# Low parts of two value-weight units formed by accumulating transfers in place of VectorE differences

## The reference, cut to what matters

```python
xn = rmsnorm(x, ln_g)
proj = xn @ w_in
q, k, v, z_a, x_b, z_b, g_a, g_b = jnp.split(proj, SPLIT_IDX, axis=-1)
q = rope(q.reshape(B, L, RET_HEADS, RET_DK), pos)
k = rope(k.reshape(B, L, RET_HEADS, RET_DK), pos) * (RET_DK ** -0.5)
v = v.reshape(B, L, RET_HEADS, RET_DV).astype(jnp.float32)
```

## Time and profile before

| | |
|---|---|
| median of 3 runs | 1920.78 us (1920.63 to 1921.49) |
| the profiled execution | 1921.01 us, of it the span 1919.2 us |
| TensorE busy | 1898.3 us, 99% of the span |
| VectorE, ScalarE, GpSimd busy | 1190.7, 771.4 and 267.1 us |
| mean granted TensorE clock | 0.998 |

### The profile page before, as it was taken

How to read it: one execution, slowest core, us unless ns; L and a number is a source line. 1 busy time by engine, 2 the same in 40 slices (tenths; PEclk the granted TensorE clock), 3 DMA queues, 4 the chain that set the end, 5 groups by cost and what they waited for, 6 DMA issues and landing times.

```text
span 1919.2 us, 32122 instructions
## 1 busy us (share of the span) xinstructions
PE 1898.3 (99%) x13128; PEld 1778.4 (93%) x13128; DVE 1190.7 (62%) x2024; ACT 771.4 (40%) x1205; POOL 267.1 (14%) x377
## 2 busy tenths in 40 slices
PE   8999999999999999999999999999999999999998
PEld 7889898898899999999998988988988999999997
DVE  8775665665766887424487656657557578763345
ACT  5432332323436776422344323234133377754223
POOL 2220120120232200000022201202102422000000
PEclk9999999999999999999999999999999999999999
DMA  6435544453453333322255445534543533342222
GB/s 217 133 118 165 171 136 129 159 179 116 138 158 97 108 99 119 103 78 78 88 172 157 143 126 170 176 113 144 171 130 126 164 108 105 92 138 79 88 79 81
DMA packets 105857, 246.99 MB, mean 129 GB/s; under 512 B 10830, under 2 KB 51262, under 8 KB 105326
## 3 DMA queue, kind: packets, MB, share of 16 engines
q1 hardware_dynamic: 78590, 149.71, 25.1%
q0 software_dynamic: 26976, 95.22, 15.0%
q10 hardware_dynamic: 144, 0.00, 0.0%
HBM read 186.07 MB, written 49.12 MB: 123 GB/s over the span
## 4 chain that ended last, share of the span: by engine, by line
PE 87%; DVE 5%; ACT 3%; DMA 1%; DVEq 1%; issue 1%; ACTq 1%; SPq 0%
PE bank L1679 22%; PE bank L1681 21%; PE bank L1680 21%; PE bank L1749 4%; PE bank L1751 4%; PE bank L1750 4%; PE last L1767 1%; PE last L1749 1%; PE last L1750 1%; PE last L1751 1%; PE sums L1874 1%; PE sums L1878 1%; PE sums L1876 1%; PE sums L1785 1%; PE bank L1932 1%
## 5 line engine op out<-in xcount | busy, mean ns | idle before, releaser
L1679 PE MATMUL bank<-xn_hi,w_hi 128*128 128x296 f32 (+1 forms) x2432 | 726.5, 299 | 0.1
L1681 PE MATMUL bank<-xn_lo,w_hi 128*128 128x296 f32 (+1 forms) x2432 | 722.3, 297 | 0.0
L1680 PE MATMUL bank<-xn_hi,w_lo 128*128 128x296 f32 (+1 forms) x2432 | 721.5, 297 | 0.0
L1679 PEld LDWEIGHTS bank<-xn_hi,w_hi 128*128 128x128 f32 x2432 | 457.3, 188 | 6.3 <-issue 4.3
L1680 PEld LDWEIGHTS bank<-xn_hi,w_lo 128*128 128x128 f32 x2432 | 457.7, 188 | 1.0
L1681 PEld LDWEIGHTS bank<-xn_lo,w_hi 128*128 128x128 f32 x2432 | 456.8, 188 | 0.0
L474 DVE TENSOR_TENSOR w_lo<-w_raw,w_hi 128x1024 fp32r<-128x1024 f32 x245 | 300.4, 1229 | 185.6 <-ACT w_hi L466 179.1
L466 ACT ACTIVATE w_hi<-w_raw 128x1024 fp32r<-128x1024 f32 x245 | 257.8, 1055 | 355.8 <-DMA w_raw<-in_w_units 351.4
L1679 PE MATMUL bank<-oa_hi,w_hi 128*128 128x296 f32 (+1 forms) x512 | 153.7, 300 | 0.0
L1680 PE MATMUL bank<-oa_hi,w_lo 128*128 128x296 f32 (+1 forms) x512 | 151.9, 297 | 0.0
L1681 PE MATMUL bank<-oa_lo,w_hi 128*128 128x296 f32 (+1 forms) x512 | 151.7, 296 | 0.0
(11 more groups left out here) (296 smaller groups left out, 3064.6 us busy)
## 6 DMA issues: line engine op xcount, KB each, us to landing
w_raw<-in_w_units SPq DMA_DIRECT2D x215, 512.0 KB, 3.6
S<-in_state_ret POOLq DMA_DIRECT2D x64, 512.0 KB, 4.8
out_ret_s<-S POOLq DMA_DIRECT2D x64, 512.0 KB, 6.0
w_raw<-in_w_units SPq DMA_DIRECT2D x66, 256.0 KB, 3.2
vst<-v_scr SPq DMA_DIRECT2D x8, 512.0 KB, 4.1
out_ret_p<-Sp POOLq DMA_DIRECT2D x8, 512.0 KB, 5.6
v_scr<-vtok_hi SPq DMA_DIRECT2D x16, 160.0 KB
dec<-in_decay POOLq DMA_DIRECT2D x9, 264.0 KB, 5.0
```

The lines of the kernel that those rows point to most:

```text
L1679: pe.matmul(ps, w_hi[:, slot, cols], x_hi, start=first, stop=False)
L1680: pe.matmul(ps, w_lo[:, slot, cols], x_hi, start=False, stop=False)
L1681: return pe.matmul(ps, w_hi[:, slot, cols], x_lo, start=False, stop=last)
```

## The change

For units 4 and 5 of the first head of the first layer alone, the low part is made in another way. After making the high part, ScalarE drains and writes the negated high part into `w_lo`. GpSimd then issues two transfers for each unit, with the same strided source as the load of `w_raw`, that add the raw weights from memory to what stands in `w_lo` (raw + (-high) = low). VectorE's `split_lo` for these units makes no difference any more; it waits for both transfers and then counts `unit_lo` up. GpSimd issues unit 4's transfers behind the four state loads, and unit 5's between the low parts of input blocks 1 and 2 (`k == 2`), each after waiting for the negated part.

```diff
+        BY_SUM = (4, 5)
+
+        def by_sum(ph, l, it, i):
+            return ph == "R" and (l, it) == (0, 0) and i + AHEAD in BY_SUM
+
         def split_hi(act, ph, l, it, i):
...
             act.activation(w_hi[:, n % RING, :], w_raw[:, n % RING, :], ACT.Copy).then_inc(unit_hi, 1)
+            if by_sum(ph, l, it, i):
+                act.drain()
+                act.activation(w_lo[:, n % RING, :], w_hi[:, n % RING, :].bitcast(f32), ACT.Copy, scale=-1.0)\
+                   .then_inc(minus_hi, 1)
+
+        def add_raw(pool, u):
+
+            pool.wait_ge(minus_hi, BY_SUM.index(u) + 1)
+            if is_value(u):
+                n = u % 16 - 4
+                for i in range(2):
+                    k = 2 * n + i
+                    pool.dma_start(w_lo[:, u % RING, i * DV:i * DV + DV].rearrange("p (c w) -> p c w", c=4),
+                                   w_units[u - n:u - n + 4, :, k * P:k * P + P].rearrange("c p w -> p c w"),
+                                   accum_op=ADD).then_inc(lo_in[BY_SUM.index(u)], 16)
...
         def split_lo(dve, ph, l, it, i):
...
+            if by_sum(ph, l, it, i):
+                dve.wait_ge(lo_in[BY_SUM.index(n)], 32 if is_value(n) else 16)
+                dve.sem_inc(unit_lo, 1)
                 return
...
                     for n in range(S_RING):
                         load_state(n)
+                    if hh == 0:
+                        add_raw(pool, BY_SUM[0])
                     if h == 0:
                         for k in range(KT):
+                            if hh == 0 and k == 2:
+                                add_raw(pool, BY_SUM[1])
                             pool.wait_ge(xnh_ready, l * KT + k + 1)
```

More of the change, by code:

```diff
@@ L369, in trunk @@
             "const_in", "trig_in", "ones_ready", "x_ready", "x_stored", "x_again"))
-        gain_in = sem("gain_in")
+        gain_in, minus_hi, lo_in = sem("gain_in"), sem("minus_hi"), [sem(f"lo_in{i}") for i in range(2)]
         xgh_ready, xg_ready = sem("xgh_ready"), sem("xg_ready")
@@ L466, in split_hi @@
             act.activation(w_hi[:, n % RING, :], w_raw[:, n % RING, :], ACT.Copy).then_inc(unit_hi, 1)
+            if by_sum(ph, l, it, i):
[11 more added lines that the diff above has]
+                                   accum_op=ADD).then_inc(lo_in[BY_SUM.index(u)], 16)
+            else:
+                pool.dma_start(w_lo[:, u % RING, :], w_units[u], accum_op=ADD).then_inc(lo_in[BY_SUM.index(u)], 16)
         def split_lo(dve, ph, l, it, i):
@@ L471, in split_lo @@
             if l * UNITS_LAYER + it * p.units + p.unit0 + n >= UNITS:
+                return
+            if by_sum(ph, l, it, i):
+                dve.wait_ge(lo_in[BY_SUM.index(n)], 32 if is_value(n) else 16)
+                dve.sem_inc(unit_lo, 1)
                 return
```

## The result

The changed kernel takes 1925.02 us (median of 11 runs, 1923.58 to 1926.50) against 1920.78 before (11 runs, 1920.22 to 1921.49): 4.2 us more, ratio 1.0025 with a 95% interval of 1.0017 to 1.0032. That is a loss, at the edge of the 0.2% that I called no change. Its first state load starts at 23.91 us against 23.55 before, so its start was 0.36 us slower for reasons outside the change; this is taken off where positions are compared.

A forecast was written before the change was run, and what follows sets the result against it. TensorE, 99% busy, was taken to bound the kernel, with 2.2 us of gaps to win. Unit 5's landing at 46.4 starts VectorE's normalisation late (44.01 before), transposes 2.4 us late: 1920.8 becomes 1923.2 us, range 1919.8 to 1927.5.

The forecast's parts named there:

- the forecast: Unit 5's transfers land at 46.4 (44.0 to 47.8), clock full, transposes 2.4 us late: 1923.2 us; chance 0.42.
- rival 2: TensorE idles 3.9 us before the third value block and its clock falls: +2.1, together +4.5, 1925.3 us; chance 0.14.
- What bounds: TensorE, 99% busy; VectorE's first normalisation at 44.01 fixes the transposes 6.17 us later, so a delay there is paid in full.
- ScalarE's copies: One added copy per unit, about 1.2 us with the drain, lies in ScalarE's idle time and costs nothing.
- Unit 4: Its transfers land by 36.9, VectorE asks at 39.9: hidden; a 1.2 us difference comes off VectorE.
- The issues: GpSimd issues unit 5's two transfers at 38.9 and 39.6, 0.71 us each, holding nobody else.
- one of my signs of being wrong: On GpSimd, the forecast is wrong if the issues take much longer than 0.7 us each.
- The landing of unit 5: Where VectorE waits: 39.6 + 3.4 + 1.7 + 1.7 = 46.4, bounds 42.3 to 49.2.
- the shared engines: Unit 7's loads, issued at 40.54, share the transfer engines and delay unit 5's landing by 1.7 us, between nothing and 1.8.
- the addition: Reading the target as well as the source delays unit 5's landing by 1.7 us, between nothing and 1.8.
- rival 1: Unit 5's addition is slow, a third of a copy's rate: landing from 47.8, loss over 0.2%, up to 1926.0; chance 0.24.
- The clock's price: At 1.2 GHz the 12 remaining value products take 2.8 us more, less 0.7 slack before the transposes: +2.1 us.

The follow-up runs named there:

- second group: Later experiments on one chip, beside 27 runs of the kernel before (1920.90 us), including the change measured again: 1924.76 us, ratio 1.0020.
- unit 5 alone: Changed kernel with unit 4's low part made by VectorE again, only unit 5's by transfers: 1925.32 us, ratio 1.0019 to the kernel before.
- kept-warm: Changed kernel plus 18 idle TensorE products between the second and third value block: 1923.82 us, measured again 1924.08.
- unit 7's loads held back: Changed kernel with SyncE waiting for unit 5's transfers before loading unit 7: 1922.80 us, ratio 1.0010 to the kernel before.

## Why the prediction was right, and where it was short

The measured time lies in the range, and the sign of the forecast, a small loss, is right. But of my cases the likeliest (landing at 46.4, clock full, 1923.2) isn't the one that came; it was rival 2, to which I had given 0.14. That its 1925.3 is so near to the measured 1925.02 is luck: the landing came later than rival 2 had it, and the clock cost less.

- *What bounds*: right. VectorE's normalisation and the transposes moved as one pattern; with the clock kept, 6.18 us apart as against 6.17.
- *ScalarE's copies*: hidden, 1.06 us each as taken. Not foreseen: unit 5's raw weights land 0.8 us late beside unit 4's addition. In unit 5's place it changed nothing, since GpSimd was busy to 39.2 anyway.
- *Unit 4*: right. Hidden; alone it gave 1.1 us in the medians, about the difference's length, though not clear of noise.
- *The issues*: one of my signs of being wrong came true. I took 0.71 us for each; unit 5's two take 1.31 and 1.80 us. The second still starts 0.80 us behind the first, so nobody on GpSimd is held, but the first byte moves some 0.5 us later than with copies.
- *The landing of unit 5*: 47.20 − 0.36 = 46.8 in the frame of before, predicted 46.4; in the second group's trace 0.3 later still (47.52 − 0.38 = 47.1). From the first issue on, my sum was 0.7 + 3.4 + 1.7 + 1.7 = 7.5; measured are 8.0 in the first trace and 8.3 to 8.6 in the other three with unshifted transfers. Within the second group the shared engines measure 2.1 (term 1.7) and the addition 2.0 (term 1.7), which leaves 4.2 for the rest (terms 0.7 + 3.4 = 4.1). Against the first trace they measure 1.8 and 1.7, and 4.5 is left. So each term is right within some 0.4 us, and which one is short isn't settled: each difference rests on single traces, and the copies share the engines with unit 7 from 1.0 us behind their first issue on, the additions from 1.7. The Trainium skill's rule ("Collectives: The Full Stack", The bandwidth ceiling), an add at half the rate of a copy, agrees with the traces: 158 to 161 GB/s against 290 to 334. That an addition goes at a third of a copy's rate, as rival 1 had it, falls.
- *The step that failed* is the choice between forecast and rival 2: "For it" had a gap of 3.9 us and a clock that fell 1.9 us after the last product at the end of the trace; "Against it" had only that the neighbouring work is dense. The runs showed that dense work on both sides doesn't save it: in all five traces in which TensorE stood idle for 2.7 us or more here (2.74, 3.58, 3.86, 4.54 and 4.85), the clock fell in the gap. It stayed full in the gap of 1.65 us that the kernel before has at 25 us:

```profile
26.81 0.37 PE L1679 MATMUL bank<-xg_hi,w_hi 128*128 128x296 f32 x1 [1.65 <-DVE qk L1201]
```

  The length of one gap alone doesn't decide, though. Near 8 us, where TensorE's work is in pieces, the clock was at half in some executions and not in others, whatever the kernel: at 0.50 with unit 5 alone, behind a gap of 1.92 us (the rows below), and in the second kept-warm trace behind gaps of 1.24 and 0.81 us, but at 1.00 in the profiles of before and of the change. Where it fell, the start was later (first state loads at 24.25 and 24.21).

```profile
6.87 0.41 PE L1707 MATMUL bank<-xg_hi,w_hi 128*128 128x296 f32 x1 [1.92 <-DVE w_lo L1119]
```

```profile
8.00:9.00 1.00, 1.00 (x5) 0.90 (x4) 0.04 (x1) 0.70 (x2) 0.00 (x0) 0.50 1.06 440
```

  The warning that I cited from the Trainium skill ("TensorE: Matmul & The Clock Gate", Why this matters for your kernels) deserved more weight than 0.14.
- *The clock's price* was mis-sized in turn: 2.1 predicted, 0.9 to 1.1 measured at the transposes. The twelve products take 4.7 to 4.9 us up to the transposes where they take 2.9 at full clock (50.22 to 52.88 and 0.23 more), so 1.8 to 2.0 us more in place of 2.8, since the clock came back before the twelfth. And the slack before the transposes is 0.9 us (53.11 to 54.01), not 0.7.

The sum of the measured terms in the second group: 2.4 forecast, + 0.8 later landing, is 3.2, what the kept-warm kernel lost. The change lost 3.9; the 0.7 between the two is the clock's price in the medians, and the 0.9 to 1.1 of the traces is near it. In the first measurement the change lost 4.2, inside the intervals (each is about 3 us wide). So the sum fits, but the last term of it comes from the two times that it explains.

What stays open: in the traces 0.4 to 0.8 us of the delay at the transposes are given back at the wait near 81 us, which was wrong in my text: there the value rows were to move with TensorE's products, and nothing behind 50.18 could absorb a delay. SyncE issues the keys' rows at 70.14 against 66.98 and the stacked values at 79.56 against 76.25, 3.2 and 3.3 us later, following VectorE, while TensorE's products before the wait are 4.3 later. The medians don't show this gift. Either the wait at 81 us is longer in the profiled execution of before than it is as a rule, or it is lost again later. Single profiles can't tell: the stretch between the transposes near 456 and those near 1404 us, the same work in all kernels, is anything from 0.9 us shorter (the change) to 0.5 us longer (unit 7's loads held back) than in the profile of before.

## What to carry to other kernels

Moving work from an engine to a transfer pays only if the engine no longer stands for it: let the consumer wait for the transfer, not the engine that was relieved. Here the same transfers cost 4 us with the wait on VectorE and won 2 with the wait on TensorE. Sum a landing from issue to wake-up with everything else that is in flight. And when the sum leaves TensorE idle, look at the length of the gap: between dense stretches each one of 2.7 us and more cost the clock here, and the one of 1.65 us did not, while in the sparser work near 8 us shorter gaps did in some executions.

## What the runs showed of the hardware

Two accumulating transfers of 256 KB in 512-byte pieces take 1.31 and 1.80 us of GpSimd's timeline as issues, where plain copies take 0.79 and 0.75, though the second starts 0.8 us behind the first in both cases. The transfer engines move about 160 GB/s while they add, against 290 to 334 while they copy, and the pair lands 1.7 to 2.0 us later than as copies.

The granted clock fell within a gap of 2.74 us between dense stretches, 2.4 us after the last product's end there and 2.0 us after it in the changed kernel. It didn't come back with the first product: in the changed kernel work resumed at 49.59 and the clock was full from 54 on, and until then products of 512 columns stood 0.43 us apart instead of 0.23.
